# Output phases and their norms over two column halves, in a two-layer fp32 hybrid trunk

## The reference

```
hx = modulate(rms_norm(x, norm1_g), sh1, sc1)        # h * (1 + scale) + shift
zx = hx @ w_in                                       # then RWKV, convolution and gating branches
m  = branches[0]*g[0] + branches[1]*g[1] + branches[2]*g[2]
x  = x + g1 * (m @ w_merge)                          # "res1"
h2 = modulate(rms_norm(x, norm2_g), sh2, sc2)
gu = h2 @ ffn_w_in
x  = x + g2 * ((silu(gu[:DFF]) * gu[DFF:]) @ ffn_w_out)   # "res2", DFF = 2816
```

## Time and profile before

| what | value |
|---|---|
| median of three runs | 4349.19 us |
| lowest and highest run | 4340.85 and 4356.56 us |
| profiled execution, its own time | 4361.62 us |
| span of the profiled execution | 4359.8 us |
| TensorE (PE) busy | 4146.8 us, 95% |
| TensorE weight loads (PEld) busy | 2420.8 us, 56% |
| VectorE (DVE) busy | 1354.8 us, 31% |
| ScalarE (ACT) busy | 1072.7 us, 25% |
| DMA over the span | 260.34 MB, mean 60 GB/s |
| mean granted TensorE clock | 0.981 of full |

### The profile page before, as it was taken

How to read it: one execution, slowest core, us unless ns; L and a number is a source line. 1 busy time by engine, 2 the same in 40 slices (tenths; PEclk the granted TensorE clock), 3 DMA queues, 4 the chain that set the end, 5 groups by cost and what they waited for, 6 DMA issues and landing times.

```text
span 4359.8 us, 107588 instructions
## 1 busy us (share of the span) xinstructions
PE 4146.8 (95%) x50580; PEld 2420.8 (56%) x50580; DVE 1354.8 (31%) x2123; ACT 1072.7 (25%) x1783; POOL 58.1 (1%) x52
## 2 busy tenths in 40 slices
PE   7999999989999999999999988999998899999998
PEld 3566666666455555555555546666665444444443
DVE  2655555555710000100000145555554310010000
ACT  3444444432110000100000244454443120010000
POOL 0000000000000000000000000000000000000000
PEclk9999999999999999999999989999998999999999
DMA  5000000103412111111111200000001442212222
GB/s 192 24 8 23 23 23 23 33 21 125 160 64 97 55 52 50 44 53 49 53 53 53 84 25 8 22 22 22 22 31 32 169 145 78 77 64 77 77 82 72
DMA packets 67383, 260.34 MB, mean 60 GB/s; under 512 B 7680, under 2 KB 9984, under 8 KB 66048
## 3 DMA queue, kind: packets, MB, share of 16 engines
q1 hardware_dynamic: 62208, 219.18, 15.3%
q10 hardware_dynamic: 3456, 29.04, 1.6%
q0 software_dynamic: 1280, 5.24, 0.3%
HBM read 239.80 MB, written 13.63 MB: 58 GB/s over the span
## 4 chain that ended last, share of the span: by engine, by line
PE 90%; ACT 4%; issue 3%; DMA 2%; DVE 1%; SPq 0%; ACTq 0%; DVEq 0%
PE psum L632 37%; PE psum L973 15%; PE psum L1340 12%; PE psum L857 11%; PE psum L869 5%; PE psum L1005 2%; PE psum L623 2%; PE psum L817 2%; DMA ring<-w_stream_in 2%; PE psum L740 1%; PE psum L835 1%; PE psum L760 1%; ACT L1391 1%; ACT arena L1729 0%; ACT arena L1722 0%
## 5 line engine op out<-in xcount | busy, mean ns | idle before, releaser
L632 PE MATMUL psum<-arena,ring 128*128 128x512 f32 (+1 forms) x4432 | 1600.3, 522 | 2.0 <-DMA ring<-w_stream_in 1.2
L632 PEld LDWEIGHTS psum<-arena,ring 128*128 128x128 f32 x4432 | 840.2, 190 | 770.3 <-issue 722.2
L973 PEld LDWEIGHTS psum<-arena 32*32 32x32 f32 (+3 forms) x40512 | 703.7, 118 | 368.7 <-issue 281.9
L973 PE MATMUL psum<-arena 32*32 32x32 f32 (+4 forms) x40512 | 795.5, 209 | 111.8 <-issue 65.4
L857 PE MATMUL psum<-arena,ring 128*128 128x512 f32 (+1 forms) x1408 | 575.2, 525 | 4.7 <-ACT arena L1541 1.6
L1340 PE MATMUL psum<-arena,ring 128*128 128x512 f32 (+1 forms) x1440 | 520.2, 521 | 0.0
L1340 PEld LDWEIGHTS psum<-arena,ring 128*128 128x128 f32 x1440 | 273.6, 190 | 242.0 <-issue 229.5
L857 PEld LDWEIGHTS psum<-arena,ring 128*128 128x128 f32 x1408 | 242.5, 192 | 165.3 <-issue 135.4
L2354 DVE TENSOR_TENSOR arena<-psum,arena 128x768 f32<-128x768 f32 (+1 forms) x44 | 36.3, 825 | 718.9 <-PE psum L632 687.2
L2296 DVE TENSOR_TENSOR arena<-psum,arena 128x768 f32<-128x768 f32 (+1 forms) x48 | 39.6, 825 | 605.8 <-PE psum L632 605.8
L1856 ACT ACTIVATE arena<-psum 128x768 f32<-128x768 f32 (+1 forms) x44 | 31.0, 704 | 698.8 <-PE psum L632 677.2
(11 more groups left out here) (123 smaller groups left out, 2560.7 us busy)
## 6 DMA issues: line engine op xcount, KB each, us to landing
ring<-w_stream_in SPq DMA_DIRECT2D x408, 512.0 KB, 3.6
x_spill<-arena ACTq DMA_DIRECT2D x2, 3072.0 KB, 8.7
arena<-ya_spill ACTq DMA_DIRECT2D x2, 3072.0 KB, 10.3
arena<-x_spill ACTq DMA_DIRECT2D x2, 3072.0 KB, 18.2
ring<-w_stream_in ACTq DMA_DIRECT2D x8, 512.0 KB, 6.2
arena<-x_in ACTq DMA_DIRECT2D x1, 3072.0 KB, 14.1
arena<-ups_in SPq DMA_DIRECT2D x16, 192.0 KB, 2.4
ya_spill<-arena POOLq DMA_DIRECT2D x8, 384.0 KB, 5.7
```

What stands on the lines that cost most here:

```text
L632: mm = eng.matmul(psum[0:lhs[k].shape[-1], tile, a - off:b - off], lhsT=lhs[k], rhs=rhs[k][:, a:b], start=(k == 0), stop=(k == len(lhs) - ...
L973: return pe.matmul(out, lhsT=lhs, rhs=rhs, start=start, stop=stop, skip_group_check=True)
```

## The change

The output phases res1 and res2 run over the columns in two sides, cut at column 512 (`CUT`): in layer 0 512 and then 256 columns, in layer 1 256 and 256. Side 0 goes through all eight blocks before side 1 begins, so the weights of these phases are streamed twice. While TensorE works on side 1, ScalarE and VectorE finish the norm and the modulation of side 0. `project_two` goes over the columns in the same two sides. The reload of ya and the sgu parameters is issued after the gelu of sv1, that of x after the gate g00, on a semaphore of its own. In the first phase the sums of squares come in three groups, `norm_rsqrt` runs before the copy of the last conditioning result, and VectorE norms side 0 before `mod_ready(0)`. The output is stored in 16 pieces instead of 8.

```diff
+CUT = 512
+FIRST_SUMS = {9: range(0, 6), 11: range(6, 12), 13: range(12, 16)}
...
+        def side_cols(c0, h):
+            return ((c0, CUT), (CUT, T))[h]
...
         def project_two(eng, tiles, chunks, rhs, c0, ready):
-            for k in range(KT):
-                eng.wait_ge(*ready(k))
-                for x in range(2):
-                    for a, b in halves(c0, c0):
+            for h in range(2):
+                a, b = side_cols(c0, h)
+                for k in range(KT):
+                    eng.wait_ge(*ready(h * KT + k))
+                    for x in range(2):
                         last[x] = eng.matmul(psum[:, tiles[x], a - c0:b - c0], lhsT=lhs[x][k], rhs=rhs[k][:, a:b],
...
 # first phase, TensorE
-                    if q >= KT:
-                        norm_sum(0, q - KT, 2, 0)
+                    for i in FIRST_SUMS.get(q, ()):
+                        norm_sum(0, i, 2, 0)
...
 # out_phase, TensorE
-                for j in range(KT):
-                    tile = j % 3
-                    take(tile, V.at(f"x{j}", l))
+                for i in range(2 * KT):
+                    h, j = divmod(i, KT)
+                    tile = i % 3
+                    a, b = side_cols(c0, h)
+                    take(tile, V.at(f"x{h}{j}", l))
...
-                            for a, b in halves(c0, c0):
-                                mm = pe.matmul(psum[:, tile, a - c0:b - c0], lhsT=w, rhs=mov[k][:, a:b],
+                            mm = pe.matmul(psum[:, tile, a - c0:b - c0], lhsT=w, rhs=mov[k][:, a:b],
...
+                    if i >= 2:
+                        norm_sum(NORMS[norm], i - 2, 3, NORM_FROM[norm])
+                for i in (2 * KT - 2, 2 * KT - 1):
+                    norm_sum(NORMS[norm], i, 3, NORM_FROM[norm])
...
 # first phase, ScalarE
+                norm_rsqrt(0, (0, 1), 2, 0)
                 act.wait_ge(*S.at(f"m0.{MOD_ITEMS - 1}"))
                 mod_copy(0)
-                norm_rsqrt(0, 2, 0)
                 act.wait_ge(*modr.at(0, 1))
-                modulated(0, 0, 0)
+                modulated(0, 0, 0, 0)
+                modulated(0, 1, 0, 0)
...
 # branch phase, ScalarE
-                act.wait_ge(s_ya, 16 * KT * (l + 1))
-                act.dma_start(arena[:, YA0 * T:(YA0 + KT) * T], ya_spill).then_inc(s_back, 16)
-                act.dma_start(arena[:, X0 * T:(X0 + KT) * T], spill).then_inc(s_back, 16)
-                act.dma_start(sgu_w, sgu_w_in[l, :, :]).then_inc(s_sgu, 16)
-                act.dma_start(sgu_b, sgu_b_in[l, :, :]).then_inc(s_sgu, 16)
...
                     gelu("sv", SV, j)
+                    if j == 1:
+                        act.wait_ge(s_ya, 16 * KT * (l + 1))
+                        act.dma_start(sgu_w, sgu_w_in[l, :, :]).then_inc(s_sgu, 16)
+                        act.dma_start(sgu_b, sgu_b_in[l, :, :]).then_inc(s_sgu, 16)
+                        act.dma_start(arena[:, YA0 * T:(YA0 + KT) * T], ya_spill).then_inc(s_back, 16)
...
                 gate("g00")
                 copied(mod_thirds(l)[1])
+                act.dma_start(arena[:, X0 * T:(X0 + KT) * T], spill).then_inc(s_x, 16)
...
+            def squares(which, l, norm, scales):
                 tables(LOG)
+                c0, n = NORM_FROM[norm], NORMS[norm]
+                for i in range(2 * KT):
+                    h, j = divmod(i, KT)
+                    act.wait_ge(*phases[which]["V"].at(f"x{h}{j}", l))
+                    square(i, c0)
+                    if i == KT:
+                        norm_rsqrt(n, (0,), 3, c0)
+                        tables(LOG)
+                    if scales is not None and KT < i <= KT + 4:
+                        if i == KT + 1 and scales:
+                            act.wait_ge(*modr.at(mod_thirds(l)[1], 1))
+                        modulated(n, 0, scales, c0, 2 * (i - KT - 1), 2 * (i - KT))
+                norm_rsqrt(n, (1,), 3, c0)
+                if scales is not None:
+                    modulated(n, 1, scales, c0)
...
 # VectorE
+            normed(0, 0, 0)
             mod_ready(0)
-            normed(0, 0)
+            normed(0, 1, 0)
...
+            def out_phase(which, l, gate, norm, scaled):
+                for i in range(2 * KT):
+                    h, j = divmod(i, KT)
...
+                    if KT < i <= KT + 4:
+                        scaled(m, 0, c0, 2 * (i - KT - 1), 2 * (i - KT))
+                scaled(m, 1, c0)
```

More of the change, by code:

```diff
@@ L330, in names_out @@
 def names_out(per):
-    return dict(PE=[f"o{j}{n}" for j in range(KT) for n in range(per)], V=[f"x{j}" for j in range(KT)])
+    return dict(PE=[f"o{h}{j}{n}" for h in range(2) for j in range(KT) for n in range(per)],
+                V=[f"x{h}{j}" for h in range(2) for j in range(KT)])
 def names_ffn():
@@ L367, in build @@
         s_spill = sem("x_spilled")
-        s_back = sem("x_reloaded")
+        s_back, s_x = sem("scan_output_reloaded"), sem("x_reloaded")
         s_ya = sem("scan_output_stored")
@@ L414, in build @@
         lora_chunks = ["w", "a", "g", "pad"]
-        res1_chunks, res2_chunks = [f"o{j}0" for j in range(KT)], [f"o{j}{n}" for j in range(KT) for n in range(3)]
+        res1_chunks, res2_chunks = names_out(1)["PE"], names_out(3)["PE"]
         phase("mod", dict(PE=[f"m0.{q}" for q in range(MOD_ITEMS)]))
@@ L604, in branch_tiles, with segs @@
             return at
-        def segs(c0):
-            return ([(0, 0, CTX)] if c0 == 0 else []) + [(1, CTX, T)]
+        def segs(a, b):
+            return [(s, max(a, lo), min(b, hi)) for s, lo, hi in ((0, 0, CTX), (1, CTX, T)) if max(a, lo) < min(b, hi)]
         def halves(c0, off):
@@ L1835, in branch_phase @@
                     act.dma_start(par[:, :], par_in[l + 1, :, :]).then_inc(s_par, 16)
-            def squares(which, l, norm):
+            def squares(which, l, norm, scales):
                 tables(LOG)
-                for j in range(KT):
-                    act.wait_ge(*phases[which]["V"].at(f"x{j}", l))
-                    square(j, NORM_FROM[norm])
-                norm_rsqrt(NORMS[norm], 3, NORM_FROM[norm])
+                c0, n = NORM_FROM[norm], NORMS[norm]
+                for i in range(2 * KT):
+                    h, j = divmod(i, KT)
+                    act.wait_ge(*phases[which]["V"].at(f"x{h}{j}", l))
+                    square(i, c0)
+                    if i == KT:
+                        norm_rsqrt(n, (0,), 3, c0)
+                        tables(LOG)
+                    if scales is not None and KT < i <= KT + 4:
[5 more added lines that the diff above has]
+                    modulated(n, 1, scales, c0)
             def ffn_phase(l):
@@ L1862, in _ @@
                 branch_phase(l)
-                squares("res1", l, ("norm2", l))
-                act.wait_ge(*modr.at(mod_thirds(l)[1], 1))
-                modulated(NORMS["norm2", l], 1, cols(l))
+                squares("res1", l, ("norm2", l), 1)
                 ffn_phase(l)
-                squares("res2", l, AFTER[l])
-                if l < DEPTH - 1:
-                    modulated(NORMS[AFTER[l]], 0, 0)
+                squares("res2", l, AFTER[l], 0 if l < DEPTH - 1 else None)
         @block.vector
@@ L2363, in _ @@
                 branch_phase(l)
-                dve.wait_ge(s_back, 32 * (l + 1))
+                dve.wait_ge(s_x, 16 * (l + 1))
                 dve.wait_ge(*modr.at(mod_thirds(l)[1], 1))
-                out_phase("res1", l, 2)
-                normed(NORMS["norm2", l], cols(l))
+                out_phase("res1", l, 2, ("norm2", l), normed)
                 ffn_phase(l)
-                out_phase("res2", l, 5)
-                if l < DEPTH - 1:
-                    normed(NORMS[AFTER[l]], 0)
-            dve.wait_ge(*nr.at(NORMS["final", 1]))
-            for j in range(KT):
-                dve.scalar_tensor_tensor(out=slot(H0 + j, CTX), in0=slot(X0 + j, CTX), scalar=par_c("fin", j), in1=slot(NT, CTX),
-                                         op0=ALU.mult, op1=ALU.mult).then_inc(xn.sem, 1)
+                out_phase("res2", l, 5, AFTER[l], normed if l < DEPTH - 1 else last_scaled)
         @block.gpsimd
@@ L2464, in weight_stream @@
                 put(np.concatenate([tile(x["conv_out"][l], j * P), tile(x["sgu_out"][l], j * P)], 1))
-        for j in range(KT):
+        for j in list(range(KT)) * 2:
             put(tile(x["w_merge"][l], j * P))
```

109 lines of the change are left out of this document (59 added, 50 removed).

## The result

The changed kernel took 4324.6 us in the median of six runs (4316.37 to 4329.03), against 4352.24 us for the kernel before in six runs. The ratio is 0.9936, 95% interval 0.992 to 0.9952. The kernel is faster by 27.6 us. The forecast was 4310.3 with a range of 4296 to 4330; the time lies in the range, the gain was forecast too large (38.9 us).

A forecast was written before the change was run, and what follows sets the result against it. TensorE bounds the kernel (90% of the span), with holes, lower clock and tail to gain; 25.4 + 11.2 + 3.3 - 1.0 = 38.9 us off the 4349.2 median gives 4310.3, range 4296 to 4330 (own terms 4298 to 4322).

The forecast's parts named there:

- Passages: From the last res matmul to project_two's end, three places: TensorE finds side 0 ready; gain 25.4 us.
- Norm of side 0 inside side 1: In res1 and res2, ScalarE and VectorE work on side 0 fits within side 1's blocks; cost 0.
- Halved matmuls: Layer 1's pairs of 256 columns instead of 512: doubled weight loads lie behind the matmul before; cost 0.
- rival of the exposed weight load: In the changed phases every additional weight load shows, costing 103 us, total 4413; chance 0.03.
- Streaming twice: In res1 and res2, 64 more chunks of 512 KB land before they are needed; cost 0.
- End: Behind the kernel's last matmul, 10.0 us instead of 13.3 for 256 columns; gain 3.3 us, bounds 2 to 5.
- First phase: Up to the first project_two: TensorE starts it near 52.8 against 51.86; loss 1.0 us, bounds 0 to 2.5.
- the 52 to 54 named as a sign: In the profile after, the first project_two would start at 52 to 54 us.
- only at 51.1 comes to mod_ready: First phase: VectorE norms side 0 from 46.2, eight times 0.6 us, before mod_ready, for which the modulation waits.
- Reloads: Branch phases: later reloads of ya, sgu and x gain 11.2 us together, bounds 4 to 13.
- 0 to 8 us of wait; I take 2, since the sgu parts come first and the chunks were issued first: Branch phase of layer 1: wait for sv3's ring chunk beside the ya and sgu reloads, taken as 2 us.
- the reload wait only moves: Layer 1: sv3's ring chunk comes last behind ya, 8 us with a slow start; gain 28.9, total 4320; chance 0.08.

The follow-up runs named there:

- e4: Changed kernel with one more wait: project_two begins only when side 1's first block is modulated; ratio 0.9968 to the kernel before.
- e3: Kernel before with the 512-column matmuls of res1 and res2 in layer 1 cut into 256 and 256, same weights; ratio 1.0002 to the kernel before.
- e7: Changed kernel with VectorE norming two blocks of side 0, then mod_ready(0), then the other six; ratio 0.9918 to the kernel before.
- e8: Changed kernel with the edits of e6 and e7, and only ya's 512 latent columns loaded in layer 1; 4309.98 us, ratio 0.99 to the kernel before.
- e10: Changed kernel run once more, unaltered; ratio 0.9928 to the kernel before.
- e2: Kernel before with only the reloads moved: sgu parameters and ya behind sv1's gelu, x behind g00; ratio 0.9992 to the kernel before.
- e9: Kernel before profiled once more, unaltered; span 4359.4 us.
- e1: Changed kernel with all reloads back at the start of the branch phase, everything else changed; ratio 0.9932 to the kernel before.
- e6: Changed kernel with sgu parameters issued behind cb2's sigmoid and ya in four two-block parts behind cb3, su3, sv0 and sv1; ratio 0.9906 to the kernel before.

## Why the prediction was right in sign and range, and where its size was off

- **Passages**: forecast 9.5 + 8.8 + 7.1 = 25.4 us, measured 9.3 + 8.6 + 6.4 = 24.3. The chain, the gap (0.16 us against 0.2) and the full clock after it came as told, and e4 shows that the wait is what the overlap removes. Of the 1.1 us that are missing, 0.4 is the pace of the halved rows in layer 1 (below). The rest is that each passage lost some 0.4 us beside its work and not 0.2: in layer 0, 22.35 us from the last matmul of res1 to the end of project_two, against 21.93 for three sums and project_two.
- **Norm of side 0 inside side 1**: cost 0 as forecast. Blocks follow at 3.885 us (1747.23 and 1751.12 in the chain of blocks of side 1), 0.015 above the forecast.
- **Halved matmuls**: forecast 0, measured 1.1 us in e3 and 1.35 us in res2 of layer 1 of the changed kernel up to its last matmul (157.58 against 156.23). Of the 1.35, 0.43 is one more sum of 256 columns that now lies ahead of the last matmul; the remaining 0.92 agrees with the 0.91 of e3 in this phase. A row of 256 columns takes 0.2159 us and not half of 0.4291. The prediction had read 0.213 from the earlier trace rows: nine loads in 1.92 us are eight steps and one load of 0.19, so 0.216 a step. The rival of the exposed weight load is refuted.
- **Streaming twice**: cost 0. In res2 of layer 1 the chunks land in 3.3 to 4.1 us (median 3.6), and no row in res1 or res2 waits for one.
- **End**: forecast 3.3, measured 3.25 behind the last matmul.
- **First phase**: forecast +1.0, measured +2.3, inside its bounds of 0 to 2.5, but at their edge: over the profiles with this first phase (e4, e7 and e8 aside) against the four with the old one it is +2.8. project_two started at 54.65, outside the 52 to 54 named as a sign. The step "only at 51.1 comes to mod_ready" came at 52.98, since the exponential was ready at 48.1 and not at 46.2. The first group of sums ran partly at the lower clock (7.12 us for twelve rows; the granted clock of 30 to 35 is 0.56). e7 shows that the order of `mod_ready` is worth more than this whole loss.
- **Reloads**: this is the mis-sized term: forecast 11.2 us, measured 4.4 (4.7 in layer 1, -0.3 in layer 0), near its lower bound of 4. All profiles together give less, and below that bound: the five with the late reloads in one burst (the changed kernel, e10, e7, e4, e2) average 396.1 us in layer 1 and 596.0 in layer 0, the four with the early ones (the kernel before, e9, e3, e1) 399.6 and 594.7, a gain of 2.3 us in all. The failed step is "0 to 8 us of wait; I take 2, since the sgu parts come first and the chunks were issued first". Two of the three chunks were issued behind the reloads, and the chunk that TensorE waited for was not that of sv3 but that of the second item behind sv2, just ahead of it. The two queues moved packet for packet, which is no even share of the bytes when one of ya's packets is 24.6 KB and one of the ring's 3.6. So 7.2 us were lost up to sv3 and 0.6 more in it. Layer 0, forecast at 0, lost 3.4 us up to sv3 (1166.68 against 1163.27), because the chunk landed after 14.3 us and not within 11.5. The rival "the reload wait only moves" was the right mechanism, as e1 and e2 show. I had given it 0.08. That its total gain of 28.9 us comes so close to the 28.3 is luck: it leaves 1.2 us of the reload term where 4.4 came, and the other terms fell short of their forecasts by 3.8 together.

With -24.3, -4.4, -3.25, +2.3 and +1.35 the sum is -28.3, against 27.6 measured. The range held because it reached to the rivals: 4324.6 lies outside the 4298 to 4322 that the forecast's own terms gave. Of the 14.3 us between it and the forecast of 4310.3, 11.3 are gain that did not come, and 3.0 are the median of the kernel before, which rose from 4349.2 (three runs) to 4352.24 (six).

## What to carry to other kernels

A norm between two dense phases costs its chain and the lower clock after it. Splitting the columns and running one side's norm behind the other side's matmuls removes both, at the price of streaming the weights twice, which was free here, with chunks landing in 3.3 to 4.1 us and no wait for one. A bulk reload that is merely moved takes its stall along: cut it into pieces with packets no longer than those of the stream beside it, and issue them one entry at a time. On an in-order engine, a small operation that others wait for belongs in front of the bulk of multiplies, at the point where its input arrives.

## What the runs showed of the hardware that I had not expected

- A DMA issue on ScalarE's queue left when the activation ahead of it started (3450.76 against 3450.75), not when it ended. In e6 the issue behind cb2's sigmoid left at 3395.80, 1.2 us before that sigmoid started (3397.03), beside the table load ahead of it.
- While two DMA queues were busy with long transfers, they moved about equal numbers of packets whatever their size: 93 and 95 in 6 us with packets of 24.6 and 3.6 KB, 261 and 250 in 4 us with 2.7 and 3.8 KB. Beside ya's packets of 24.6 KB a 512 KB chunk landed after 13.3 and 14.2 us; with 2.7 KB packets and the same bytes, 10.2 at most.
- In e4, 3.58 idle us were followed by matmuls that took 1.9 us longer (granted clock 0.69 in the window). The 0.16 us gaps of the changed kernel left the clock at 1.00.
